# Weight sums of a fast matrix product: three of eight moved from accumulating DMA to GpSimd

## What is computed

```python
h = rms_norm(x, pre_g)
qc, kc, vc, gc, qd, kd, vd, gd = _split(h @ w_in, ODD_IN_WIDTHS)
qc = partial_rope(qc, pos); kc = partial_rope(kc, pos)
oc = dilated_mixture_attention(qc, kc, vc)      # three groups, window/dilation (128,1) (512,4) (2048,16)
od, lse = banded_attention(qd, kd, vd, 128)     # with a sink logit per head
mix = concat([oc * silu(gc), od * silu(gd)])
return x + rms_norm(mix @ w_out, post_g)
```

## The kernel before

| op | 0 1 | 2 3 | 4 5 | 6 | 7 8 | 9 10 | 11 | 12 13 | 14 | 15 16 | 17 |
|---|---|---|---|---|---|---|---|---|---|---|---|
| name | W11 | V0 V1 | P | W21 0 | W22 | Q | V2 | R | W21 1 | T | V3 |
| buffer | 0 1 | 2 3 | 0 1 | 4 | 2 3 | 0 1 | 4 | 2 3 | 4 | 0 1 | 2 |

## Times and profile before

### The profile page before, as it was taken

One profiled execution on the slowest core, in us unless ns is written; L12 is line 12 of the kernel. 1 busy time (PEld: TensorE's weight loads), 2 busy tenths in 40 slices (PEclk: granted clock), 3 DMA queues, 4 the chain that ended last, 5 costly groups with the idle time before them and its releaser, 6 DMA issues.

```text
span 1224.0 us, 15110 instructions
## 1 busy us (share of the span) xinstructions
PE 1183.8 (97%) x5660; PEld 986.8 (81%) x5660; DVE 784.4 (64%) x937; ACT 621.7 (51%) x854; POOL 120.6 (10%) x165
## 2 busy tenths in 40 slices
PE   7999999999999999999999999898998979999997
PEld 6788888888888888788888888786786868888886
DVE  5375546566666954777555558685886858667654
ACT  5554443545545543665445456464565655445442
POOL 2400001200000000010000001310213113000000
PEclk9999999999999999999999999998998999999999
DMA  9994443444445555654445389799797988434541
GB/s 367 254 310 173 166 177 137 176 168 142 172 166 206 201 193 195 229 209 177 172 152 192 137 243 211 267 248 276 235 230 257 252 221 358 158 138 172 176 168 69
DMA packets 39206, 249.39 MB, mean 204 GB/s; under 512 B 4928, under 2 KB 5056, under 8 KB 11632
## 3 DMA queue, kind: packets, MB, share of 16 engines
q1 hardware_dynamic: 31248, 201.34, 45.4%
q0 software_dynamic: 7040, 45.13, 16.7%
q10 hardware_dynamic: 864, 2.18, 0.5%
HBM read 244.44 MB, written 4.19 MB: 203 GB/s over the span
## 4 chain that ended last, share of the span: by engine, by line
PE 74%; DMA 16%; DVE 4%; ACT 3%; issue 2%; POOL 1%; SPq 0%; ACTq 0%; DVEq 0%
PE acc L517 63%; DMA g_turned<-weights 8%; DMA raw<-weights 6%; DVE w_lo L1483 3%; PE bank_x L667 2%; PE acc L724 2%; DMA probs<-x_nat 2%; ACT w_hi L1013 1%; PE bank_x L651 1%; PE bank_y L621 1%; PE acc L735 1%; PE bank_x L597 1%; PE bank_y L597 1%; ACT w_hi L841 0%; ACT w_hi L1001 0%
## 5 line engine op out<-in xcount | busy, mean ns | idle before, releaser
L517 PE MATMUL acc<-w_hi,act_hi 128*128 128x512 f32 x1176 | 466.2, 396 | 2.5 <-DVE w_lo L1186 2.5
L517 PE MATMUL acc<-w_lo,act_hi 128*128 128x512 f32 x1176 | 458.9, 390 | 0.0
L1186 DVE TENSOR_TENSOR w_lo<-raw,w_hi 128x2048 fp32r<-128x2048 f32 x147 | 337.8, 2298 | 161.5 <-ACT w_hi L841 161.3
L841 ACT ACTIVATE w_hi<-raw 128x2048 fp32r<-128x2048 f32 x147 | 281.7, 1916 | 156.4 <-PE acc L517 130.2
L517 PE MATMUL acc<-w_hi,act_lo 128*128 128x512 f32 x1176 | 315.1, 390 | 0.1
L517 PEld LDWEIGHTS acc<-w_hi,act_hi 128*128 128x128 f32 x1176 | 221.1, 188 | 46.9 <-DVE w_lo L1186 3.7
L517 PEld LDWEIGHTS acc<-w_hi,act_lo 128*128 128x128 f32 x1176 | 220.6, 188 | 47.2 <-DVE act_lo L1195 0.5
L517 PEld LDWEIGHTS acc<-w_lo,act_hi 128*128 128x128 f32 x1176 | 221.2, 188 | 42.9
L1483 DVE TENSOR_TENSOR w_lo<-raw,w_hi 128x1024 fp32r<-128x1024 f32 x104 | 125.6, 1246 | 14.8 <-ACT w_hi L1013 14.1
L1013 ACT ACTIVATE w_hi<-raw 128x1024 fp32r<-128x1024 f32 x104 | 104.5, 1051 | 24.8 <-DMA raw<-weights 22.2
L863 ACT ACTIVATE probs<-scores,negm 128x256 f32<-128x256 f32 (+1 forms) x80 | 36.5, 458 | 98.6 <-DVE negm L1273 73.3
(11 more groups left out here) (223 smaller groups left out, 1113.6 us busy)
## 6 DMA issues: line engine op xcount, KB each, us to landing
raw<-weights SPq DMA_DIRECT2D x175, 1024.0 KB, 4.8
raw<-weights POOLq DMA_DIRECT2D x32, 1024.0 KB, 12.0
g_turned<-weights SPq DMA_DIRECT2D x24, 512.0 KB, 9.9
resid<-x_turned SPq DMA_DIRECT2D x8, 256.0 KB, 9.3
mix<-rpb POOLq DMA_DIRECT2D x32, 64.0 KB, 23.8
postg<-post_g POOLq DMA_DIRECT2D x2, 1024.0 KB, 26.7
resid<-x_perm POOLq DMA_DIRECT2D x2, 1024.0 KB, 8.2
x_kept<-resid POOLq DMA_DIRECT2D x2, 1024.0 KB, 4.3
```

The source lines that it names most:

```text
L517: m = nc.tensor.matmul(tiles[t][:, :], a[:, kt, t * P:(t + 1) * P], w[:, buf, kk * NB:(kk + 1) * NB], start=(kt == 0 and a is act_hi and w ...
L841: nc.scalar.activation(w_hi[:, at % SPLIT, :], raw[:, at % RAW, :], ACT.Copy).then_inc(S["hi_ready"], 1)
L1186: nc.vector.tensor_tensor(w_lo[:, at % SPLIT, :], raw[:, at % RAW, :], w_hi[:, at % SPLIT, :].bitcast(F32), ALU.subtract).then_inc(S["lo_r ...
```

## The change

Q 0, Q 1 and T 1 are now made by GpSimd `tensor_tensor` additions. Q needs chunks 6 and 7, which are also W22 and lie in buffers 2 and 3; T 1 needs chunk 3, which is W21 1 and lies in buffer 4. P, R and T 0 stay accumulating DMAs. R's DMAs overwrite buffers 2 and 3 and so now wait for Q's additions (`q_added`); the next load into buffer 4 waits for T 1's (`t_added`). ScalarE waits for the same semaphores before it splits Q and T 1.

```diff
-FAST_SUMS = ("P", "Q", "R", "T")
+BY_DMA = (("P", 0), ("P", 1), ("R", 0), ("R", 1), ("T", 0))
+BY_POOL = (("Q", 0), ("Q", 1), ("T", 1))
@@ SP
                     load(3, d + 9, op + 14)
+
+                    sp.wait_ge(S["t_added"], k + 1)
                     load(4, d + 2, op + 15)
@@ GpSimd
-                        for o, chunk in ((4, 4), (5, 5), (9, 6), (10, 7), (12, 4), (13, 5), (15, 2), (16, 3)):
+                        k = u.body - FAST0
+
+                        def add_weights(o, chunk):
+
                             r = FAST_RAW[o]
                             before = max(n for n in range(o) if FAST_RAW[n] == r)
                             pool.wait_ge(S["lo_ready"], op + before + 1)
                             pool.dma_start(raw[:, r, :], weights[d + chunk], accum_op=ALU.add).then_inc(added[r], 16)
+
+                        add_weights(4, 4)
+                        add_weights(5, 5)
+                        for c in range(2):
+
+                            pool.wait_ge(S["lo_ready"], op + 5 + c)
+                            pool.wait_ge(landed[2 + c], fast_landings(k, 7 + c))
+                            pool.tensor_tensor(raw[:, c, :], raw[:, c, :], raw[:, 2 + c, :], ALU.add).then_inc(
+                                S["q_added"], 1)
+                        for c in range(2):
+
+                            pool.wait_ge(S["q_added"], 2 * k + c + 1)
+                            add_weights(12 + c, 4 + c)
+                        add_weights(15, 2)
+
+                        pool.wait_ge(S["lo_ready"], op + 11)
+                        pool.wait_ge(landed[4], fast_landings(k, 14))
+                        for half in range(2):
+                            m = pool.tensor_tensor(raw_part(1, half), raw_part(1, half), spare[half], ALU.add)
+                        m.then_inc(S["t_added"], 1)
@@ ScalarE
-                        if FAST_OPS[n][0] in FAST_SUMS:
+                        if FAST_OPS[n][0] == "Q":
+                            act.wait_ge(S["q_added"], 2 * k + FAST_OPS[n][1] + 1)
+                        elif FAST_OPS[n] in BY_POOL:
+                            act.wait_ge(S["t_added"], k + 1)
+                        elif FAST_OPS[n] in BY_DMA:
                             act.wait_ge(added[FAST_RAW[n]], fast_sums(k, n))
```

More of the change, by code:

```diff
@@ L68 @@
 FAST_SLOTS = [(o, x) for o, (name, _) in enumerate(FAST_OPS) for x in ((0, 1) if name == "V" else (None,))]
-FAST_SUMS = ("P", "Q", "R", "T")
-FAST_COUNT = [sum(r == raw and name not in FAST_SUMS for raw, (name, _) in zip(FAST_RAW, FAST_OPS))
+BY_DMA = (("P", 0), ("P", 1), ("R", 0), ("R", 1), ("T", 0))
+BY_POOL = (("Q", 0), ("Q", 1), ("T", 1))
+FAST_COUNT = [sum(r == raw and op not in BY_DMA + BY_POOL for raw, op in zip(FAST_RAW, FAST_OPS))
               for r in range(RAW + 1)]
-FAST_ADDED = [FAST_RAW.count(r) - FAST_COUNT[r] for r in range(RAW)]
+FAST_ADDED = [sum(r == raw and op in BY_DMA for raw, op in zip(FAST_RAW, FAST_OPS)) for r in range(RAW)]
 ALL_OPS = ALL_CHUNKS + FAST * (FAST_N - BODY)
@@ L95, in fast_sums @@
     r = FAST_RAW[o]
-    mine = sum(FAST_RAW[n] == r and FAST_OPS[n][0] in FAST_SUMS for n in range(o + 1))
+    mine = sum(FAST_RAW[n] == r and FAST_OPS[n] in BY_DMA for n in range(o + 1))
     return 16 * (FAST_ADDED[r] * k + mine)
@@ L101, in fast_landings @@
     r = FAST_RAW[o]
-    mine = sum(FAST_RAW[n] == r and FAST_OPS[n][0] not in FAST_SUMS for n in range(o + 1))
+    mine = sum(FAST_RAW[n] == r and FAST_OPS[n] not in BY_DMA + BY_POOL for n in range(o + 1))
     return 16 * (RING + FAST_COUNT[r] * k + mine) if r < RAW else 32 * (FAST_COUNT[r] * k + mine)
@@ L299, in build @@
                  "rs_v rs_s rs_rdy tanh_done gate_u gate_done q_zeroed "
-                 "kept s_sum s_raw s_hi s_lo hi_half lo_half half_used n1_taken n5_taken n6_taken c11_taken").split()
+                 "kept s_sum s_raw s_hi s_lo hi_half lo_half half_used n1_taken n5_taken n6_taken c11_taken q_added t_added").split()
         S = {n: sem(n) for n in names}
```

## The result

The changed kernel takes 1240.45 us (1239.61 to 1243.17) against 1227.45 (median of four executions; the 1227.87 of the table above is that of three of them): a ratio of 1.0104 (95% interval 1.0081 to 1.0128), 13 us slower. The forecast was 1222.8 us with a range of 1201 to 1239. The whole loss lies in the four fast bodies.

What follows compares the result with a forecast made beforehand. Slow loads into buffer 4 were taken to bound the fast bodies, above PE's 65.2 us; DVE's sum gave -1.2 us for three later bodies and -3.9 for the first: 1227.87 - 5.1 = 1222.8 us, range 1201 to 1239.

Steps and rivals of the forecast that it cites:

- The relief: In the fast bodies, removing three accumulating loads per body lets them shrink toward PE's 65.2 us: at most 33 us.
- The additions: GpSimd needs 4.6 us for a Q addition, 2.4 us for each half of T 1, 14.0 us per body.
- The hold: DVE and GpSimd wait for each other's whole instructions, in turns; DVE is held 12.2 us per body.
- V2's load: Load into buffer 4: lands in some 6 us, under 8 as the sign, instead of 15.71; V2's wait goes.
- W21 1's load: Beside R 1 and T 0 but not T 1, takes 8.5 to 9 us, not 12.36; over 10 means forecast wrong.
- the sum on DVE: DVE's work, held time and waits: 74.8 us per later body instead of 75.2, 68.2 in the first instead of 72.1.
- The second rival: Delayed R 1 and T 0 slow W21 1's load; T 1's additions alternate with W21 1's splits: 1238 us, chance 0.25.
- some 3 us of standing at W21 0: PE stands some 3 us at W21 0 and spends there what V2's wait gave back.

## Why the prediction was wrong

- The relief. Up to 33 us by PE's own time; 28.5 measured. Right.
- The additions. 4.6 and 2.4 us; 4598 ns median for the one, 2394 at least for the other. Right.
- The hold. Whole instructions, in turns, 12.2 us per body; DVE's busy time rose by 11.5, and in the run with memsets, which read nothing, it stayed at 224.2 us for the four bodies. Eleven subtractions lasted over 3 us, where nine to twelve were expected. Right.
- V2's load. Under 8 us expected; two halves of 512 KB landed after 4.3, and DVE no longer waits before V2. Right.
- W21 1's load. 8.5 to 9 us; 9.92 in the chain of the second body, 10.7 to 11.1 in the others, which the text had named as a sign that it is wrong. The load was taken 1 to 2 us too short, for a reason that was only half seen: R and T 0 do come late (by 9 us of the body, where 7 were expected), but as the end of a hole of 12 us in the DMA engines' work.
- The step that failed is the sum on DVE. It added held time to DVE's work and then gave DVE almost no idle time: 5.2 us in a later body, 3.5 in the first. Measured are 9.2, 12.0 and 10.0, and 11.7 in the first (length less busy time in the windows above). That is 4.0 + 6.8 + 4.8 + 8.2, some 24 us, less 3 by which DVE's busy time was taken too high: the bodies were forecast at 292.6 us and came to 313.5. DVE was treated as if it could run ahead whenever work was left, so that a hold would use up idle time. In this kernel no engine can: VectorE may lead TensorE by two operands, SP loads only after VectorE's split, TensorE waits for VectorE's bank reads. Q 0's hold uses up the lead (TensorE waits for P 1, 0.53 us), Q 1's then stops TensorE for 3.74 us, and it starts again at half rate. That VectorE afterwards waits for TensorE and for the late loads, and so keeps its idle time, is read from the waits in the code and from the hole in the DMA row; no run with more buffers has tested it.
- The wait that was not named: PE before T 0 on line 1543, a bank read queued behind two held splits. It stands in the code and shows no idle time in the trace of before. Moving that read gives back 4 of the 13 us.
- The second rival named 1238 us, near the measured time, and that is in part luck. Its mechanism was there in part: W21 1's load took over 10 us in three bodies, and T 1's additions and W21 1's splits did take turns (5.74 and 5.85 us in the listings). But the rival charged its extra time to T 1's additions, and these by themselves left the kernel 6.4 us faster than before. Of the 42 us by which the four bodies are longer than without the sums (313.5 against 271.3), the stops at W21 0 with their slow matmuls are about 17, those before T 0 as much again. The text had seen some 3 us of standing at W21 0 and booked them against V2's wait; it had no term for slow matmuls after a stop.

Open: the third body is longer than its neighbours (75.8 us before, 81.8 after, 70.0 without the sums). In all three traces TensorE waits there, and in no other body so long, for VectorE's copy into `g_turned` in the attention (1.48, 1.22 and 1.80 us); no run looked for the reason. How much of Q's price is the hole in the DMA engines and how much TensorE's stops was not separated.

## What to carry over

Before moving elementwise work to GpSimd, ask whether it reads SBUF while VectorE runs two-operand instructions: then its time is VectorE's time, and idle time on VectorE was no cover here, with buffers for a lead of two operands (whether more buffers would make it one was not tested). Where every engine waits for the next one (a ring of buffers), a first estimate adds the hold to the length of the loop, not to one engine's budget: here 3.7, 7.3 and 11.2 us of hold cost 2.8, 6.8 and 10.2. Take the parts of a change one by one: here one of three sums was worth keeping (T 1, ratio 0.9942), and the other two cost about three times its gain.

## What the hardware showed

- 13 memsets of 128x256 on GpSimd, 4.75 us together, left VectorE's subtractions at 1.2 us; one addition of 128x2048, 4.6 us, stretched one of them to 5.65 us.
- VectorE's `tensor_scalar` on two elements, with one SBUF input, was held too when it met Q 0's addition in the fourth body: 3.61 us, where such an operation took 0.17 us in the kernel before.

```profile
974.10 3.61 DVE L1303 TENSOR_SCALAR negm<-rmax 128x2 f32<-128x2 f32 x1
```

- With the additions in place the DMA engines stood still for about 12 us of the second body, without them for 5: the loads wait for VectorE's splits.
- After PE had stood for 3.74 us, its matmuls of 512 columns started 0.43 us apart for about 4 us (granted clock 0.50), then 0.227 again; a stop of 2.20 us was followed by slow matmuls too. In the run without the sums the granted clock of all four bodies was 1.00, in the changed kernel 0.93 to 0.98.
